# Cutting the chunk stages of a recurrence into pieces between the k steps of dense products

## The reference

```
p = h @ w_in                                    # (T, 3*512 + q 256 + k 256 + v 512 + o 512 + gates 8)
u = cg * xin ;  y = conv_b + width-3 causal conv of u ;  a = group_rmsnorm(bg * y)
# mLSTM, 4 heads, chunk by chunk (carry C, n, m):
s   = (q k^T) * exp(d_log - m_t)
num = s v + w_inter * (q C) ;  den = sum(s) + w_inter * (q n)
h   = num / max(|den|, exp(-m_t))
C, n = decay * C + sum(wk k v^T), decay * n + sum(wk k)
hm  = rmsnorm(h) * sigmoid(o)
out = concat(a, hm) @ w_out
```

## Time and profile before

| what | value |
|---|---|
| median of 3 runs | 2126.74 us (2124.0 to 2131.44) |
| span of the profiled execution | 2134.3 us |
| PE busy | 2053.9 us, 96% |
| DVE busy | 949.9 us, 45% |
| ACT busy | 515.4 us, 24% |
| POOL busy | 106.9 us, 5% |

### The profile page before, as it was taken

How to read it: one execution, slowest core, us unless ns; L and a number is a source line. 1 busy time by engine, 2 the same in 40 slices (tenths; PEclk the granted TensorE clock), 3 DMA queues, 4 the chain that set the end, 5 groups by cost and what they waited for, 6 DMA issues and landing times. The chain is left out here.

```text
span 2134.3 us, 31347 instructions
## 1 busy us (share of the span) xinstructions
PE 2053.9 (96%) x12605; PEld 2022.3 (95%) x12605; DVE 949.9 (45%) x1598; ACT 515.4 (24%) x908; POOL 106.9 (5%) x141
## 2 busy tenths in 40 slices
PE   6799999999999998999999889999999999999996
PEld 5799999999999998999999879999999999999996
DVE  6633323432333348412666655633333433343247
ACT  4311111111111125322333331412112211112123
POOL 2100000000000012000000011100000000000012
PEclk8899999999999999998999989999999999999998
DMA  6011011110111011311110240121011101111002
GB/s 200 1 60 59 20 39 59 59 53 23 43 59 59 10 63 40 82 40 30 31 30 29 102 94 21 40 60 60 20 39 59 59 20 39 59 59 59 0 1 82
DMA packets 144037, 104.60 MB, mean 49 GB/s; under 512 B 6361, under 2 KB 136233, under 8 KB 143977
## 3 DMA queue, kind: packets, MB, share of 16 engines
q1 hardware_dynamic: 143976, 103.77, 16.0%
HBM read 94.83 MB, written 8.92 MB: 49 GB/s over the span
## 5 line engine op out<-in xcount | busy, mean ns | idle before, releaser
L219 PE MATMUL bank<-in_hi,w_hi 128*128 128x352 f32 x2256 | 744.5, 330 | 22.2 <-DVE in_lo L166 11.8
L225 PE MATMUL bank<-in_hi,w_lo 128*128 128x352 f32 x2256 | 733.1, 325 | 0.0
L224 PE MATMUL bank<-in_lo,w_hi 128*128 128x352 f32 x2256 | 731.6, 324 | 0.0
L219 PEld LDWEIGHTS bank<-in_hi,w_hi 128*128 128x128 f32 x2256 | 430.0, 191 | 28.5 <-issue 10.1
L224 PEld LDWEIGHTS bank<-in_lo,w_hi 128*128 128x128 f32 x2256 | 432.2, 192 | 1.3
L225 PEld LDWEIGHTS bank<-in_hi,w_lo 128*128 128x128 f32 x2256 | 430.0, 191 | 0.0
L394 DVE TENSOR_TENSOR ffn_hidden<-ffn_silu,bank 128x352 f32<-128x352 f32 x132 | 68.8, 521 | 658.0 <-PE bank L225 581.2
L219 PE MATMUL bank<-ffn_hidden_hi,ffn_w_hi_more 128*128 128x352 f32 x1056 | 343.7, 325 | 13.0 <-issue 11.9
L405 DVE SCALAR_TENSOR_TENSOR x<-bank,x 128x352 f32<-128x352 f32 x528 | 267.5, 525 | 167.5 <-PE bank L225 114.8
L225 PE MATMUL bank<-ffn_hidden_hi,ffn_w_lo_more 128*128 128x352 f32 x924 | 298.3, 323 | 0.0
L224 PE MATMUL bank<-ffn_hidden_lo,ffn_w_hi_more 128*128 128x352 f32 x924 | 298.0, 323 | 0.0
(11 more groups left out here) (196 smaller groups left out, 1623.0 us busy)
## 6 DMA issues: line engine op xcount, KB each, us to landing
raw<-in_ffn_w_gate SPq DMA_DIRECT2D x44, 512.0 KB, 4.0
ffn_raw_more<-in_ffn_w_down SPq DMA_DIRECT2D x44, 512.0 KB, 5.6
raw<-in_w_in SPq DMA_DIRECT2D x24, 512.0 KB, 3.9
raw<-in_ffn_w_up SPq DMA_DIRECT2D x22, 512.0 KB, 5.0
ffn_raw_more<-in_ffn_w_up SPq DMA_DIRECT2D x22, 512.0 KB, 5.5
x_parked<-x SPq DMA_DIRECT2D x3, 1408.0 KB, 5.6
x<-x_parked SPq DMA_DIRECT2D x3, 1408.0 KB, 11.0
raw<-in_w_out SPq DMA_DIRECT2D x8, 512.0 KB, 3.8
```

The lines of the kernel that those rows point to most:

```text
L219: pe.matmul(out, w_hi, in_hi, start=first, stop=False)
L224: pe.matmul(out, w_hi, in_lo, start=False, stop=False)
L225: return pe.matmul(out, w_lo, in_hi, start=False, stop=last)
```

## The change

PE's stages become generators that yield after each piece. `product` takes such a generator as `between` and asks it for one piece behind each k step, from step `start` on; `rest` issues what is left. Stage A has six pieces (v, k and rows, two of logs, two of scores), stage B six (four heads, two updates), stage C one, which comes at the second request; the columns have seven. With that each stage goes half a product or more later than it stood: A(even) within cg(0) rather than behind it means that its pieces follow k steps 0 to 5; A(odd) moves from behind xin(0) into xin(1) (from step 4) and xin(2); B(even) from behind cg(2) into cg(2) (from step 4) and xin(0); B(odd) from behind bg(0) into bg(1) (from step 2); the stage C parts into cg(1) and bg(0); the columns into tile 10's first block, A(0) into its third, B(0) into tile 11's second. The waits that a stage makes go with its pieces. On DVE u_of(1) moves ahead of stage_a(odd), and stage_c(even) behind next_low(1) and conv. No matmul is added or taken away.

```diff
 # DVE, conv tile
                 u_of(0)
+                u_of(1)
                 stage_a(odd, CHUNK)
-                u_of(1)
                 u_of(2)
-                stage_c(even, c * (2 * CHUNK), CHUNK)
                 next_low(1)
                 conv()
+                stage_c(even, c * (2 * CHUNK), CHUNK)
                 z_of(0)
 # PE
-            def product(b, j, bank=None):
+            def product(b, j, bank=None, between=(), start=0):
+                between = iter(between)
                 for k in range(KT):
...
-                last.then_inc(s.dense_done, 1)
+                    if k == KT - 1:
+                        last.then_inc(s.dense_done, 1)
+                    if k >= start:
+                        next(between, None)
+
+            def rest(pieces):
+                for _ in pieces:
+                    pass
...
             def stage_c(g, n):
+                yield
                 turn_back(pe, g, n)
...
-                cg(0)
-                stage_a(even, c * (2 * CHUNK), CHUNK)
-                cg(1)
-                if first:
-                    stage_c(0, DEC_SEQ)
-                else:
-                    stage_c(c * 2, CHUNK)
-                cg(2)
-                stage_b(even, CHUNK, state_p)
+                even_a, odd_a = (stage_a(g, c * (2 * CHUNK) + i * CHUNK, CHUNK) for i, g in enumerate((even, odd)))
+                even_b, odd_b = (stage_b(g, CHUNK, state_p) for g in (even, odd))
+                cg(0, even_a)
+                rest(even_a)
+                cg(1, stage_c(0, DEC_SEQ) if first else stage_c(c * 2, CHUNK), 1)
+                cg(2, even_b, 4)
                 pe.wait_ge(m.w_low, c * 3 + (QKVO_TILES + 3))
-                xin(0)
-                stage_a(odd, c * (2 * CHUNK) + CHUNK, CHUNK)
-                xin(1)
-                xin(2)
-                stage_c(even, CHUNK)
+                xin(0, even_b)
+                rest(even_b)
+                xin(1, odd_a, 4)
+                xin(2, odd_a)
+                rest(odd_a)
                 pe.wait_ge(m.w_low, c * 3 + (QKVO_TILES + 4))
-                bg(0)
-                stage_b(odd, CHUNK, state_p)
-                bg(1)
+                bg(0, stage_c(even, CHUNK), 1)
+                bg(1, odd_b, 2)
+                rest(odd_b)
                 stats(0)
                 bg(2)
                 stats(1)
                 stats(2)
...
-            pe.wait_ge(s.state_in, 16 * 2 * HEADS)
-            stage_a(0, SEQ, DEC_SEQ)
-            qkvo_tile(QKVO_TILES - 2, 1)
-            stage_b(0, DEC_SEQ, state_s)
-            qkvo_tile(QKVO_TILES - 1, 2)
+            def sample_a():
+                pe.wait_ge(s.columns_ready, 2)
+                pe.wait_ge(s.constants, 7)
+                pe.wait_ge(s.state_in, 16 * 2 * HEADS)
+                yield from stage_a(0, SEQ, DEC_SEQ)
+
+            qkvo_tile(QKVO_TILES - 2, 1, (columns(), (), sample_a()))
+            qkvo_tile(QKVO_TILES - 1, 2, ((), stage_b(0, DEC_SEQ, state_s), ()))
```

More of the change, by code:

```diff
@@ L1629, in _, with qkvo_tile @@
                 product(b, 1, first_banks[1][b])
-            def qkvo_tile(n, j):
+            def qkvo_tile(n, j, between=((), (), ())):
                 pe.wait_ge(m.w_low, n + 2)
@@ L1634, in qkvo_tile @@
                     pe.wait_ge(s.qkvo_copied, n * 3 + (b - 2))
-                    product(b, j)
+                    product(b, j, between=between[b])
+                    rest(between[b])
             qkvo_tile(2, 2)
@@ L1642, in _, with columns @@
             qkvo_tile(QKVO_TILES - 3, 0)
[L1644 to L1657, removed]
+            def columns():
+                pe.wait_ge(s.row_exp, 6)
+                pe.wait_ge(s.row_step, ROW_STEPS)
+                for g in range(GROUPS):
+                    t0, n = (SEQ, DEC_SEQ) if g == 0 else ((g - 1) * CHUNK, CHUNK)
+                    for kind, r in enumerate((ROW_A, ROW_WK, ROW_ENM)):
+                        at = (g * KINDS_COL + kind) * HEADS
+                        pe.transpose(num_bank[0:n, at:at + HEADS], rows[0:HEADS, r, t0:t0 + n],
+                                     sh.ident[0:HEADS, 0:HEADS])
+                        if (g * KINDS_COL + kind) % 4 == 3:
+                            yield
+                for p in range(PAIRS):
+                    last = pe.matmul(score_bank[:, p * GROUPS:(p + 1) * GROUPS], sh.pair_rows[:, p, :], decay_row[:, :],
+                                     start=True, stop=True)
+                last.then_inc(s.columns_done, 1)
             def stage_a(g, t0, n):
@@ L1678, in stage_a @@
                     last = pe.matmul(out, sh.ident16[0:n, 0:n], sh.mask[0:n, 0:n], start=False, stop=True)
-                last.then_inc(s.logs_done, 1)
+                    if h == HEADS - 1:
+                        last.then_inc(s.logs_done, 1)
+                    if h % 2:
+                        yield
                 if not (isinstance(g, int) and g == 0):
@@ L1684, in stage_a @@
                                      staged_q[:, h, 0:n], start=True, stop=True)
-                last.then_inc(s.scores_done, 1)
+                    if h == HEADS - 1:
+                        last.then_inc(s.scores_done, 1)
+                    if h % 2:
+                        yield
             def stage_b(g, n, state):
@@ L1700, in stage_b @@
                                      values[0:n, 2 * p:2 * p + 2, :], start=True, stop=True)
-                last.then_inc(s.nums_done, 1)
+                    if p == 1:
+                        last.then_inc(s.nums_done, 1)
+                    yield
             def stage_c(g, n):
+                yield
                 turn_back(pe, g, n)
@@ L1707, in conv_tile, with cg @@
                 even, odd = c * 2 + 1, c * 2 + 2
-                def cg(b):
+                def cg(b, between=(), start=0):
                     if first:
@@ L1713, in cg, with xin, bg @@
                         pe.wait_ge(s.group_mean, c * 3 + (b - 2))
-                    product(b, 0)
-                def xin(b):
+                    product(b, 0, between=between, start=start)
+                def xin(b, between=(), start=0):
                     pe.wait_ge(s.cg_copied, c * 3 + (b + 1))
-                    product(b, 1)
-                def bg(b):
+                    product(b, 1, between=between, start=start)
+                def bg(b, between=(), start=0):
                     pe.wait_ge(s.u_made, c * 3 + (b + 1))
-                    product(b, 2)
+                    product(b, 2, between=between, start=start)
                 def stats(b):
```

## The result

| kernel | median | all runs | ratio to before, 95% interval |
|---|---|---|---|
| before | 2126.70 us | 2124.0 to 2131.44 (6) | |
| after | 2141.35 us | 2136.65 to 2145.48 (6) | 1.0058 [1.0038, 1.0077] |

The change costs 14.65 us, 0.7% by the medians and 0.6% by the ratio. 2135.4 was forecast, between 2121.5 and 2145: the sign is right and the size is 6 us short.

The account below looks back on a forecast made before the run. It took TensorE (PE), busy 96% of the span, as the bound. -1.1 - 1.9 + 4.5 + 6.4 + 3.1 + 1.7 - 20 + 16 = +8.7 us on 2126.7 gave 2135.4 us, range 2121.5 to 2145.

Parts of the forecast that it names:

- step 2: Stage A and the columns: PE pauses between 4-row and 128-row matmuls, 15 round trips at 0.3 us, +4.5 us.
- Step 6: Columns through conv tiles: 20 us of old clock losses go, 16 us of new ones come with the pieces.
- the forecast's own band of +4 to +13: Whole kernel: the main case, +4 to +13 us by how often the clock falls; chance 0.50.
- more falls than before: Conv tiles: new waits and spread thin work add one 1.7 us clock fall per tile, +15.5 us, 2142.2; chance 0.15.
- Step 1: Odd and sample's stage A: PE's waits for DVE's state update and for the columns go, -1.9 and -1.1 us.
- Step 3: Odd stage B, four conv tiles: PE waits 1.6 us each for DVE's stage_c, now behind low and conv, +6.4 us.
- Step 4: Tile 3's last stats: z_of(1) comes late behind seven in_lo subtractions, and the output phase waits for it, +3.1 us.
- Step 5: First cg(0): PE waits for ACT's copy of the last qkvo tile's first block, behind stage_b(0), +1.7 us.
- The credit of 20: Columns through conv tiles: all the old clock falls go, -20 us, counted from the granted shares of one profile.
- the 16 of new falls: Columns through conv tiles: the clock falls again in the new order, 1.7 us nine to ten times, +16 us.
- the clock stays up: Columns through conv tiles: 2.4 GHz holds throughout, without new falls, sum -7.3 us, 2119.4 us; chance 0.22.
- No wait for `mixed`: Odd stage B: DVE reaches stage_c before PE gets there, the 6.4 us go, sum +2.3, 2129.0 us; chance 0.13.

Follow-up runs that it names:

- experiment 3: The changed kernel with the prompt's stage A issued whole, the even one behind cg(0), the odd one behind xin(1); 2131.54 us, ratio 1.0018.
- Experiment 5: The changed kernel with the last tile's seven L883 subtractions and ACT's high halves moved behind z_of(2), the squares and group means; 2139.31 us.
- experiment 1: The kernel before, unchanged, run and profiled once more; 2127.02 us, ratio 0.9997.
- experiment 4: The kernel before with the logs' mask added once for all four heads, as one matmul ahead of the eight 4-row matmuls; 2114.91 us.
- experiment 2: The changed kernel with stage_c(even) on DVE put back ahead of next_low(1) and conv; 2132.1 us, ratio 1.0011.
- experiments 8 and 10: Changed kernel with stage_c(even) first, last tile's subtractions later, sample's stage B earlier, one grouped mask matmul: 2114.59 us; the same with stage A whole: 2115.28 us.
- experiment 9: The kernel before with the mask added once for all heads and the odd stage A whole behind xin(1), u_of(1) ahead of it on DVE; 2114.16 us.

## Why the prediction was right in its sign and short in its size

The mechanism held in steps 1 to 5, with one term put at nothing that was not: the sample's stage B in pieces, 1.1 us (step 2). Step 6, on which the sum hung most, came out near its net by two terms that no run can size one by one. The measured +14.65 lies above the forecast's own band of +4 to +13. The number nearest to it is the +15.5 of the rival "more falls than before", and that rival's mechanism is wrong (step 6).

**Step 1, waits that go (-3.0): right.** Both waits were on L1664, now L1674, and that line is not in the list after.

**Step 2, gaps between shapes (+4.5): right for stage A and the columns, and short by the sample's stage B.** PE's timeline of A(even) in conv tile 0 of the new kernel:

```profile
994.17 0.60 PE L1674 MATMUL bank<-ident,mix_staged_kv 128*128 128x128 f32 x4
...
995.41 0.71 PE L1681 MATMUL bank<-mix_row_inter,pair_rows 4*128 4x128 f32 x4
996.04 0.43 PE L219 MATMUL bank<-in_hi,w_hi 128*128 128x352 f32 x1
...
996.72 0.48 PE L1689 MATMUL bank<-mix_row_max,head_row 4*128 4x128 f32 x2
...
997.75 0.41 PE L219 MATMUL bank<-in_hi,w_hi 128*128 128x352 f32 x1
```

The k step between two pieces of 4 rows takes 0.68 us, 996.04 to 996.72, where a k step in a product takes 0.49. The odd stage A of tile 1, in pieces and at the full clock, with its five k steps in between:

```profile
1081.11:1088.22 7.11, 7.11 (x47) 5.74 (x45) 5.91 (x9) 3.70 (x9) 0.00 (x0) 1.00 0.01 3
```

7.11 less 5 x 0.49 is 4.66, against 4.26 for the whole one of experiment 3: 0.4. By the tiles (54.7 against 54.17 for two) it is 0.3. The columns' pieces show the same in the timeline:

```profile
957.76 0.41 PE L1660 MATMUL bank<-ident,mix_rows 4*128 4x4 f32 x4
...
958.78 0.41 PE L1660 MATMUL bank<-ident,mix_rows 4*128 4x4 f32 x4
```

One comes every 1.02 us, 0.49 of it the k step. From the first to the end of the seventh are 6.18 us (956.87 to 963.05), less six k steps 3.25, and the 27 transposes took 1.60 before (957.67 to 959.27): 1.6 go to changes of shape.

The pieces of the prompt's stage B cost nothing, as costed: the even one of tile 1 runs from 1070.79 to 1075.67, 4.88 us, less five k steps 2.44, and 2.47 whole. Step 2 had the same for the sample's stage B, but that one has matmuls with 32 rows (`32*32` and `32*128` in the trace). The window table, whole before, and in pieces with five k steps after:

```profile
977.82:981.57 3.75, 3.75 (x22) 1.75 (x21) 1.23 (x1) 1.41 (x2) 0.00 (x0) 1.00 0.00 0
979.48:986.82 7.34, 7.34 (x37) 3.97 (x36) 0.00 (x0) 0.00 (x0) 0.00 (x0) 1.00 0.23 67
```

7.34 less 2.44 is 4.90, against 3.75: 1.1 us for nothing but the cutting up. Nine times 0.4, 1.6 and 1.1 make 6.3, or 5.4 with 0.3 a stage.

**Step 3, the wait for `mixed` (+6.4): right**, 6.5 in the list. The timelines of DVE and PE behind xin(2) of tile 1:

```profile
1091.81 0.58 DVE L1493 TENSOR_TENSOR mix_rows<-mix_rows,bank 128x320 f32<-128x320 f32 x2 [2.55 <-PE bank L225]
1092.46 1.22 DVE L785 TENSOR_TENSOR w_lo<-raw,w_hi 128x1024 fp32r<-128x1024 f32 x1
...
1097.45 1.12 DVE L1457 SCALAR_TENSOR_TENSOR x<-bank,vectors,mix_o_gate 128x128 f32 x4
```

```profile
1092.61 0.60 PE L1600 MATMUL bank<-ident,mix_h_tok 128*128 128x128 f32 x4
...
1098.72 0.46 PE L1714 MATMUL bank<-mix_values,mix_probs 128*128 128x129 f32 x2 [1.63 <-DVE x L1457]
```

DVE passes u_of(2), low and conv exactly as in the earlier trace rows, stage_c ends at 1098.57, and PE, which has done its three k steps of bg(1), stands 1.63.

**Step 4, stats (+3.1): the mechanism right, its place as named, the size near.** In tile 3:

```profile
1227.74 2.28 PE L1748 MATMUL bank<-mix_rows,mean_group 128*128 128x352 f32 x4 [3.50 <-ACT mix_rows L1234]
```

The prediction's 1.4 "waits" before stats(2) is the distance between two starts, and the wait in it is 0.61; the sum does not change by that. From the end of bg(2), 1224.24 by the wait, to the end of stats at 1230.02 are 5.8 us, and 2.2 before (1218.98 to 1221.21): +3.5. In the other tiles the waits are 0.9 us shorter than they were (2.5 - 0.6 = 1.9 before, 4.5 - 3.5 = 1.0 after). Net +2.6. Experiment 5 added what step 4 lacked: the place of the seven subtractions hardly matters, since DVE's whole queue has to be through.

**Step 5, first cg(0) (+1.7): right**, 1.8, ahead of the product's first matmul (993.62).

Together -3.0 + 6.3 + 6.5 + 2.6 + 1.8 = +14.2 (13.3 with 0.3 a stage), where steps 1 to 5 had +12.7. The runs show +14.7 full. The rest is within what the bookkeeping can be trusted for.

**Step 6, the clock (-20 + 16): the net was 1.6 us too good, and its two terms stay open.** The credit of 20 was read from one execution. Its listing gives

```profile
core 0: 2134.3 us, clock 0.972
```

which is 59.8 us lost, 8.2 more than the mean of 51.6. I had noticed that its span lay 7.6 above the median and turned that into a shift of scale, where it was a warning on this very term. How much of the 8.2 lies in the stretch, the runs don't say: they come with one mean clock each, and the profiles scatter outside the stretch too. Ahead of the columns, where all kernels do the same work, the twelve profiles lose from 15.4 to 20.5 us.

In the stretch, from the first column to the last tile's idle tail, the window table has for before, for experiment 1 and for after

```profile
957.67:1224.15 266.48, 258.12 (x1546) 240.93 (x1545) 150.82 (x323) 97.90 (x220) 12.93 (x24) 0.92 0.15 44
956.54:1221.36 264.82, 256.27 (x1546) 239.27 (x1545) 150.81 (x323) 98.02 (x221) 12.93 (x24) 0.92 0.15 45
956.87:1228.22 271.35, 258.38 (x1541) 233.07 (x1540) 150.24 (x321) 92.72 (x217) 12.93 (x24) 0.95 0.14 44
```

Counted from the traces' granted clock, PE is at the half level for 44.4 us in ten falls before, for 41.0 in eight in experiment 1, and for 27.3 in five after. Half of that is lost: 22.2, 20.5 and 13.7. So the two profiles of before bear the credit of 20 out, and the 16 of new falls was some 2 too large. By them 7 to 8.5 us were won in the stretch; the means over the runs show 2.4 won in all, where the step had 4. That the net of two terms from one profile came so near to the runs' is luck.

Of the 6 us by which the forecast was short, 2.0 are in the full part and 1.6 in the clock. The other 2.3 are the six runs of before beside the new kernel, which were faster than the 50 over which the means go.

Of the rivals, "the clock stays up" was wrong: the share in tiles 0 to 2 is 0.94, as forecast. The Trainium skill (TensorE: Matmul & The Clock Gate, Loop structure matters more than you think) has it that matmuls which follow one another without a break keep the clock. Here the trace doesn't agree, as far as it shows idle time: PE was busy for all of the 6.80 us from 1057.50 to 1064.30 and for all of the 5.36 us ahead of them. But the pauses between shapes count as busy in it, and the work there is full of them. The falls go with that work: experiment 4 changed only stage A's shapes, left every wait of the stretch where it was, and lost 42.3 in place of 51.6. Whether it is the pauses or the thin matmuls, no run tells apart. "No wait for `mixed`" was wrong in this kernel and is what experiment 2 built: 2129.0 forecast for it, 2132.1 measured. "More falls than before" was wrong: there are five in the stretch where there were ten.

**What stays open.** In experiment 3 pieces of stage A cost 9 us of lost clock against whole ones in the new kernel, or less, as far as part of it is gaps. In experiments 8 and 10 there is no such difference. Why the falls come with pieces when the mask is in four, and from one execution to the next at different places (experiment 3's even stage A at 1.00, that of before at 0.79), the runs don't say.

## What to carry to other kernels

Price a fine interleaving by the shape changes and by the waits of every stage that it makes later, on all queues, and only then by the clock. Where a term is a granted clock, profile the kernel twice or compare its runs' mean clocks before giving the term a size: here the span of one program moves by 13 us, mostly with its clock, as much as the change did. And look at the small work itself before moving it: putting four mask matmuls into one was worth 12 us with nothing moved, while moving and cutting the large stages, with most of the new waits repaired, was worth none. Last, follow PE's saved time to the next DMA that it meets: in experiment 9 a wait for a weight tile took most of it back.

## What the runs showed of the hardware that I had not expected

- One program's granted clock varies from run to run, 0.972 to 0.979 over the runs of experiment 1, and its span with it, 2133.6 to 2121.4 us.
- PE fell to the half level for 6.80 us with no idle time in the trace there or in the 5.36 us ahead (the rows from 1052.14), behind pieces of transposes and 4-row matmuls.
- Three changes between 4-row and 128-row matmuls fewer in each stage A took 0.6 us from each at the full clock, and in all 9.3 us of lost clock from the kernel.
- Pieces with 32-row matmuls between k steps cost 1.1 us over six pieces, pieces with 128-row matmuls none (4.90 against 3.75 us, and 2.44 against 2.47).
- Behind a wait of 10.1 us the first product of the output phase ran for 5.82 us at 0.50.
